# Forget-gate bias of eight attention heads: from prepared mask tiles on VectorE to one more accumulated matmul per score block on TensorE

## The chip, the cores and the metric

One Trainium2 chip, one of its cores. The metric is device microseconds of the whole program, the median of several runs. Engines are written as the profile writes them: PE is TensorE's matmul stream and PEld its weight load, DVE is VectorE, ACT is ScalarE, POOL is GpSimd, SP is SyncE.

## The reference, cut to what matters

The program is a four-layer model over 256 tokens of width 1024, in fp32: two layers of a first block (attention and a gated feed-forward each), then two layers of a second block with a mixture of experts. The change touches the first layer's attention alone. It has 16 heads of 64 columns: eight "dilated" heads whose bias is a constant table, and eight "forgetting" heads, whose bias depends on the data:

```python
def forgetting_attention(q, k, v, logf):
    c = jnp.cumsum(logf, axis=1)          # per token and head
    ck = jnp.transpose(c, (0, 2, 1))
    ...
        bias = jnp.transpose(cb, (0, 2, 1))[..., :, None] - ck[:, :, None, :]
        p = causal_block_probs(qb, k, start, bias)   # softmax(q.k + bias), causal
        return jnp.einsum('bqhd,...->...', p, v)
```

The term of the query's own token is the same along a softmax row and drops out, so the kernel needs only the row vector `-c` over the keys for each of the eight heads.

## The kernel before, in words

All weights stream once from memory in chunks of 128 x 2048 fp32 through a ring of three buffers. SP issues a chunk's load once the chunk three before it has been split. Each weight is split into a high part (ACT, line 350) and a low part (DVE, line 704), and `group` on PE forms each product from three fp32r matmuls (`product`, lines 1238 to 1242). The order of work on each engine is written out by hand, and the engines meet at semaphores.

The first layer's input projection runs in six groups g = 0..5 of two chunks (`projections`: ACT from line 414, DVE from 1087, PE from 1328). Between the two chunks of groups 1 to 4, PE transposes the finished query or key columns (`qk_transposes`, line 1312). The two score blocks of heads 0 and 1 start in group 5.

The forget-gate row vectors `f_w[4]` (8 heads on 8 partitions, 256 keys) are ready early: a scan on DVE at line 1075 signals `negc_ready`. Then, in groups 2 and 3, `forget_rows` on PE (line 1316) spreads four heads' rows over 128 partitions each: a matmul with one column of the identity, broadcast to 8 x 128, as stationary operand and `f_w[4]` as moving operand. `forget_masks` on DVE (line 1078) adds the constant causal mask and writes a 128 x 384 mask tile per head (lines 1084 and 1085). Those tiles lie in buffers that are free at that time.

Attention goes head by head, software-pipelined by hand. PE's `rest` (line 1380) does for head a: `scores(a + 2)`, `turn(a + 1)` (three transposes of the probabilities, line 1363), `values(a)` (lines 1372 to 1374). A head's scores are two blocks in one bank, 128 x 128 and 128 x 256, contracted over the head's 64 rows (line 1355). A head is on partitions 0..63 if even, 64..127 if odd (`head_rows`, line 1635). DVE's `scores` (line 758) adds the mask, negates and takes the row minimum in one operation per block (line 763); ACT's `softmaxes` takes the exponential and the row sum (line 396); DVE copies the turned probabilities (line 774) and scales the output (line 794). The same code serves the second attention layer (`attention(16, ...)`, 64 rows, values of 128 columns) and the second block's latent attention (96 rows, values of 64 columns).

An fp32 matmul stands in the profile as two rows, and so does its weight load; they are called two passes in what follows.

Of the kernel before, what the change touches and what calls it, by code (L numbers as in the profile page):

```python
# [20 lines left out]
ALU = mybir.AluOpType  # L21
# [3 lines left out]
P = 128  # L25
S = 256
# [85 lines left out]
def build(nc, x, stream, router, small, const, fgain, out):  # L112
    es = ExitStack()
    with es:
# [3 lines left out]
        def sem(name):  # L118
            return es.enter_context(nc.semaphore(name))
# [49 lines left out]
        f_w = [s[:, i * S:(i + 1) * S] for s, i in ((spare_c, 1), (spare_c, 2), (spare_s, 0), (spare_s, 1),  # L169
                                                    (spare_c, 0), (spare_s, 2))]  # L170

        rope_flat, stick_flat = (a[:, :, :].rearrange("p t d -> p (t d)") for a in (rope_a, sT))
        forget_mask = [zm[:, i, :] for i in range(4)] + [a[:, i * 384:(i + 1) * 384] for a in (rope_flat, stick_flat) for i in range(2)]

        spare_q = qk_tok[:, :, :].rearrange("p t d -> p (t d)")
        rw = spare_q[:, 0:384].rearrange("p (j n) -> p j n", j=24)
        rbig = spare_q[:, 512:512 + NT * NE].rearrange("p (t n) -> p t n", t=NT)
# [27 lines left out]
        h_ready, bank_done = sem("h_ready"), sem("bank_done")  # L205
        dve_step, act_step = sem("dve_step"), sem("act_step")
        qk_tok_ready, qk_tr, qkT_ready, v_ready = map(sem, ("qk_tok_ready", "qk_transposed", "qkT_ready", "v_ready"))
        rows_done, fmask_ready = sem("forget_rows_done"), sem("forget_mask_ready")
        f_z, f_neg, f_ln, negc_ready = map(sem, ("forget_z_ready", "forget_neg_ready", "forget_ln_ready", "neg_c_ready"))
        s_done, nm_ready, p_ready, p_tr, pT_ready, pv_done, o_done = map(sem, (  # L210
            "scores_done", "neg_max_ready", "probs_ready", "probs_transposed", "probsT_ready", "pv_done", "o_done"))
# [474 lines left out]
        def _(dve):  # L686
# [68 lines left out]
            def attention(first, n, masks, scale, dv, diff, between=None, score_bank=0, turned_bank=6):  # L755


                def scores(a):
                    dve.wait_ge(s_done, first + a + 1)
                    if a >= 2:  # L760
                        dve.wait_ge(p_ready, first + a - 1)
                    for t, lo, hi in ((0, 0, 128), (1, 128, 384)):
                        ins = nc.vector.tensor_tensor_reduce(  # L763
                            sm[:, a % 2, lo:hi], B[score_bank + a % 2][:, lo:hi], masks(a)[:, lo:hi], -scale, 3e38,
                            ALU.add, ALU.min, nmax[:, a, t:t + 1])
                    ins.then_inc(nm_ready, 1)

                def probs(a):
                    dve.wait_ge(p_tr, first + a + 1)
                    step[0] += 1  # L770
                    nc.vector.reciprocal(rden[:, a, :], den[:, a, :]).then_inc(dve_step, 1)
                    if a >= 2:
                        dve.wait_ge(pv_done, first + a - 1)
                    nc.vector.tensor_copy(prT[:, a % 2, :], B[turned_bank + a % 2][:, 0:384]).then_inc(pT_ready, 1)

                    if diff and a % 2:
                        dve.wait_ge(dve_step, step[0])
                        step[0] += 1
                        ts(rden[:, a, :], rden[:, a, :], lamb[:, 6:7], None, ALU.mult).then_inc(dve_step, 1)
                    scale_step[a] = step[0]  # L780

                def outputs(a):
                    dve.wait_ge(dve_step, scale_step[a])
                    dve.wait_ge(pv_done, first + a + 1)
                    if diff and a % 2:
                        dve.wait_ge(o_done, first + a)
                    for t in range(NT):
                        z = B[4 + a % 2][:, t * dv:(t + 1) * dv]
                        col = (a // 2 if diff else a) * dv
                        o = tok[:, t, col:col + dv]  # L790
                        if diff and a % 2:
                            ins = stt(o, z, rden[:, a, t:t + 1], o, ALU.mult, ALU.add)
                        else:
                            ins = ts(o, z, rden[:, a, t:t + 1], None, ALU.mult)
                    ins.then_inc(o_done, 1)

                scale_step = {}

                def start():
                    scores(0)  # L800
                    scores(1)

                def rest():
                    probs(0)
                    for a in range(n):
                        if a + 2 < n:
                            scores(a + 2)
                        if a + 1 < n:
                            probs(a + 1)
                        outputs(a)  # L810
                        if between is not None:
                            between(a)
                    dve.wait_ge(o_done, first + n)

                return start, rest
# [259 lines left out]
            nc.vector.tensor_tensor_scan(f_w[4], f_w[2], f_w[5], 0.0, ALU.mult, ALU.add)\  # L1075
                .then_inc(negc_ready, 1)

            def forget_masks(first):

                for i in range(first, first + 4):  # L1080
                    if i % 2 == 0:
                        dve.wait_ge(rows_done, i // 2 + 1)
                    rows = B[4 + i // 2 % 2][:, i % 2 * S:(i % 2 + 1) * S]
                    tt(forget_mask[i][:, 0:P], rows[:, 0:P], cs("causal", 0, P), ALU.add)
                    tt(forget_mask[i][:, P:384], rows, cs("causal", P, 384), ALU.add).then_inc(fmask_ready, 1)

            def projections(c0, qk_first, kinds, start, between=None):
                for g in range(6):
                    c = c0 + 2 * g
                    split(c + AHEAD)  # L1090
                    if g == 5:
                        start()
                    split(c + 1 + AHEAD)
                    if between is not None and g in (2, 3):
                        between(4 * (g - 2))
                    if g < 4:
                        kinds(g, qk_first + g, c + 1, 2 * (g % 2))

# [6 lines left out]
            def kinds1(g, n, c, banks):  # L1105
                rope(n, c, banks, *(("cos_q", "sin_q"), ("cos_k", "sin_k"))[g % 2])

            start, rest = attention(0, 16, lambda a: cs("dilated") if a < 8 else forget_mask[a - 8], 1.0, HD, False)
            projections(C_HYB, 0, kinds0, start, forget_masks)
            dve.wait_ge(fmask_ready, 8)  # L1110
            rest()
            nc.vector.engine_nop().then_inc(tok_ready, 2)
            low(T_L0O, xl, xh, one)
# [9 lines left out]
            dve.wait_ge(lam_exp, 1)  # L1123
            link(tt(lamb[:, 5:6], lamb[:, 3:4], lamb[:, 2:3], ALU.subtract))
            link(ts(lamb[:, 6:7], lamb[:, 5:6], -LAM_INIT, None, ALU.add))
            start, rest = attention(16, 16, lambda a: cs("causal"), 1.0, P, True, head_norms)
            projections(C_DIFF, 4, kinds1, start)
            rest()
            head_norms(17)
# [9 lines left out]
            for l in range(LAYERS):  # L1139
# [74 lines left out]
                        dve.wait_ge(spv_done, l + 1)  # L1214
                        nc.vector.tensor_copy(tok[:, :, 512:768], B[7][:, :].rearrange("p (t d) -> p t d", t=NT))

                start, rest = attention(32 + 8 * l, 8, lambda a: cs("chunked"), MLA_SCALE, HD, False, other_outputs, 2, 0)
                start()
                rest()
                nc.vector.engine_nop().then_inc(tok_ready, 2)  # L1220
# [14 lines left out]
        def _(pe):  # L1235
# [77 lines left out]
                                                  src[:, t, j * width:(j + 1) * width], ident)  # L1313
                    ins.then_inc(qk_tr, 1)

            def forget_rows(first):

                if first:
                    pe.wait_ge(fmask_ready, first)
                else:  # L1320
                    pe.wait_ge(negc_ready, 1)
                for i in range(first, first + 4):
                    row = ident[0:8, i:i + 1].broadcast_to([8, P])
                    ins = mm(B[4 + i // 2 % 2][:, i % 2 * S:(i % 2 + 1) * S], row, f_w[4], start=True, stop=True)
                    if i % 2:
                        ins.then_inc(rows_done, 1)

            def projections(c0, n0, q, start, between=None):
                for g in range(6):
                    if g == 1:  # L1330
                        pe.wait_ge(f_z, 1)
# [5 lines left out]
                    for j in group(c0 + 2 * g, 2, [B[b][:, :], B[b + 1][:, :]], 512, q if g == 0 else None):  # L1337
                        if j == 0 and 1 <= g <= 4:
                            qk_transposes(n0 + g - 1)
                        if j == 0 and g in (2, 3) and between is not None:  # L1340
                            between(4 * (g - 2))
                        if j == 0 and g == 5:
                            pe.wait_ge(qkT_ready, 2 * (n0 + 4))
                            pe.wait_ge(v_ready, n0 + 2)
                            start()

            def attention(first, n, operands, v_of, dv, between=None, score_bank=0, turned_bank=6):

                def scores(a):
                    if a >= 2:  # L1350
                        pe.wait_ge(nm_ready, first + a - 1)
                    o = B[score_bank + a % 2]
                    q, k = operands(a)
                    for lo, hi, t in ((0, 128, 0), (128, 384, 1)):
                        ins = mm(o[:, lo:hi], q[:, t * P:(t + 1) * P], k[:, 0:hi - lo], start=True, stop=True)  # L1355
                    ins.then_inc(s_done, 1)

                def turn(a):
# [277 lines left out]
                r = (a % 2) * HD  # L1636
                return qT[r:r + HD, a // 2, :], kT[r:r + HD, a // 2, :]

            start, rest = attention(0, 16, head_rows, lambda a, t: v[:, t, a * HD:(a + 1) * HD], HD)
            projections(C_HYB, 0, None, start, forget_rows)  # L1640
            pe.wait_ge(v_ready, 4)
            rest()
            pe.wait_ge(const_in, 16)
# [17 lines left out]
            for l in range(LAYERS):  # L1661
# [106 lines left out]
                def latent_heads(a):  # L1768
                    if a in (0, 4):
                        pe.wait_ge(qkT_ready, 2 * (n + (4 if a == 0 else 5)))  # L1770
                    return qT[0:MLA_QK, a, :], kT[0:MLA_QK, a, :]

                start, rest = attention(32 + 8 * l, 8, latent_heads, lambda a, t: v[:, t, a * HD:(a + 1) * HD], HD,
                                        other_mixers, 2, 0)
                start()
                qk_transposes(n + 4, MLA_QK, mla_tok[1])
# [192 lines left out]
```

## Time and profile before

| | us |
|---|---|
| runs | 1594.02, 1612.99, 1613.31 |
| median | 1612.99 |
| the profiled execution's own time | 1594.02 |
| span of the profile, first to last instruction | 1592.3 |
| what lies around the span | 1.7 |

The three runs lie in two places, 19 us apart, and the profiled execution is the shortest of them. A duration read from the profile belongs to that one.

The page's first part gives the busy time of each engine, its second part 40 slices of the span, its fourth the chain of work that ended last. A span with PE busy all through and a chain that lies on PE says that PE's own order of work sets the end there. Idle time of another engine in such a stretch costs nothing.

### The profile page before, as it was taken

The page shows a single profiled execution, that of the slowest core. Times are in us where ns is not written, and L with a number is a line of the kernel's source. Part 1 is how long each engine was busy: PE and PEld are TensorE (multiplying, and loading weights), DVE is VectorE, ACT ScalarE, POOL GpSimd, SP SyncE. Part 2 cuts the span into 40 slices and gives each one's busy share as a digit, 9 for nine tenths or more (in the row PEclk, how much of TensorE's full clock was granted, in tenths as well). Part 3 has the DMA queues.
Part 4 walks back from the last instruction along what each step waited for, and adds up shares of the span by engine and source line. Part 5 has one row for each costly group of instructions (what it writes and reads, how often), then busy time and mean ns, then how long its engine had stood idle before and what let it go on. Part 6 is the DMA issues. An engine that isn't in the chain of part 4 may idle for free.

```text
span 1592.3 us, 23360 instructions
## 1 busy us (share of the span) xinstructions
PE 1503.7 (94%) x8132; PEld 1272.6 (80%) x8132; DVE 1143.2 (72%) x1885; ACT 929.0 (58%) x1522; POOL 32.5 (2%) x68
## 2 busy tenths in 40 slices
PE   7999999999999999989879999999899799999997
PEld 5877999988778999977768887878678678787875
DVE  6665756667676656656668888889666578888886
ACT  5354554454555544547447767777555367776774
POOL 0000000000010000010000000000000000000000
PEclk9999999999999999989979999999997899999999
DMA  7422444545314454441318979799421359898984
GB/s 308 179 80 80 185 184 176 193 158 185 133 54 159 165 205 184 163 158 54 132 62 339 368 293 367 296 357 344 193 103 43 142 220 358 312 349 313 349 326 186
DMA packets 46828, 336.77 MB, mean 211 GB/s; under 512 B 5344, under 2 KB 5472, under 8 KB 6432
## 3 DMA queue, kind: packets, MB, share of 16 engines
q1 hardware_dynamic: 46656, 335.49, 56.0%
q8 instruction: 44, 0.72, 0.2%
q0 software_dynamic: 96, 0.30, 0.1%
q14 instruction: 32, 0.26, 0.1%
HBM read 334.72 MB, written 1.05 MB: 211 GB/s over the span
## 4 chain that ended last, share of the span: by engine, by line
PE 86%; DVE 6%; ACT 4%; issue 2%; POOL 1%; DMA 1%; DVEq 0%; ACTq 0%; SPq 0%; POOLq 0%
PE bank L1240 24%; PE bank L1242 23%; PE bank L1241 23%; DVE w_low L704 2%; PE bank L1355 2%; PE bank L1465 2%; PE bank L1476 2%; PE bank L1363 1%; ACT w_high L350 1%; PE bank L1508 1%; PE bank L1288 1%; ACT tok L360 1%; PE bank L1299 1%; PE bank L1312 1%; PE bank L1374 1%
## 5 line engine op out<-in xcount | busy, mean ns | idle before, releaser
L704 DVE TENSOR_TENSOR w_low<-raw,w_high 128x1024 fp32r<-128x1024 f32 (+2 forms) x630 | 734.7, 1212 | 189.9 <-ACT w_high L350 187.9
L350 ACT ACTIVATE w_high<-raw 128x1024 fp32r<-128x1024 f32 (+2 forms) x630 | 623.5, 1044 | 113.3 <-PE bank L1242 71.1
L1240 PE MATMUL bank<-w_high,x_high 128*128 128x512 f32 (+1 forms) x928 | 376.2, 405 | 8.4 <-DVE rope_b L975 3.1
L1242 PE MATMUL bank<-w_high,x_low 128*128 128x512 f32 (+1 forms) x928 | 364.0, 392 | 0.0
L1241 PE MATMUL bank<-w_low,x_high 128*128 128x512 f32 (+1 forms) x928 | 362.1, 390 | 0.0
L1240 PEld LDWEIGHTS bank<-w_high,x_high 128*128 128x128 f32 x928 | 175.7, 189 | 47.2 <-issue 9.1
L1242 PEld LDWEIGHTS bank<-w_high,x_low 128*128 128x128 f32 x928 | 175.5, 189 | 38.2
L1241 PEld LDWEIGHTS bank<-w_low,x_high 128*128 128x128 f32 x928 | 176.1, 190 | 34.4 <-issue 1.4
L1240 PE MATMUL bank<-x_high,w_high 128*128 128x256 f32 (+1 forms) x712 | 201.8, 283 | 1.0 <-DVE x_low L724 0.5
L1242 PE MATMUL bank<-x_high,w_low 128*128 128x256 f32 (+1 forms) x712 | 201.3, 283 | 0.0
L1241 PE MATMUL bank<-x_low,w_high 128*128 128x256 f32 (+1 forms) x712 | 201.3, 283 | 0.0
L1240 PE MATMUL bank<-w_high,hid_high 128*128 128x512 f32 x432 | 171.3, 397 | 1.9 <-DVE hid_low L979 1.9
L1241 PE MATMUL bank<-w_low,hid_high 128*128 128x512 f32 x432 | 170.6, 395 | 0.0
L1242 PE MATMUL bank<-w_high,hid_low 128*128 128x512 f32 x432 | 170.4, 394 | 0.0
L1240 PEld LDWEIGHTS bank<-x_high,w_high 128*128 128x128 f32 (+1 forms) x712 | 135.6, 190 | 3.8 <-DVE x_low L724 1.6
L1241 PEld LDWEIGHTS bank<-x_low,w_high 128*128 128x128 f32 (+1 forms) x712 | 135.6, 190 | 0.8
L1242 PEld LDWEIGHTS bank<-x_high,w_low 128*128 128x128 f32 (+1 forms) x712 | 135.6, 191 | 0.2
L1240 PEld LDWEIGHTS bank<-w_high,hid_high 128*128 128x128 f32 x432 | 81.4, 188 | 19.8 <-DVE hid_low L979 2.3
L1242 PEld LDWEIGHTS bank<-w_high,hid_low 128*128 128x128 f32 x432 | 81.4, 189 | 19.2
L1241 PEld LDWEIGHTS bank<-w_low,hid_high 128*128 128x128 f32 x432 | 81.5, 189 | 17.6
L396 ACT ACTIVATE probs<-scores_masked,neg_max 128x128 f32<-128x128 f32 x96 | 42.8, 446 | 55.6 <-DVE neg_max L763 55.5
L498 ACT ACTIVATE hid_high<-bank 128x256 fp32r<-128x256 f32 x64 | 24.6, 384 | 76.4 <-PE bank L1508 76.3
(244 smaller groups left out, 1434.5 us busy)
## 6 DMA issues: line engine op xcount, KB each, us to landing
raw<-stream SPq DMA_DIRECT2D x314, 1024.0 KB, 4.8
const_sb<-const SPq DMA_DIRECT2D x1, 2070.0 KB, 15.0
residual<-x SPq DMA_DIRECT2D x2, 512.0 KB, 4.3
final_gain<-fgain SPq DMA_DIRECT2D x2, 512.0 KB, 10.6
out<-residual SPq DMA_DIRECT2D x2, 512.0 KB, 2.6
small_sb<-small SPq DMA_DIRECT2D x1, 765.0 KB, 6.7
rope_a<-router POOLq DMA_DIRECT2D x2, 144.0 KB, 2.6
const_sb<-const SPq DMA_DIRECT2D x1, 136.0 KB, 4.5
```

The costliest lines, as they stand in the source:

```text
L350: nc.scalar.activation(wh[:, u, cols], raw[:, u, cols], ACT.Copy).then_inc(w_high, 1)
L360: nc.scalar.activation(tok[:, t, cols], h[:, t, cols], ACT.Square, scale=float(D) ** -0.5, accum_out=ssq[:, t, half:half + 1]).then_inc(ss ...
L396: ins = nc.scalar.activation(pr[:, a % 2, lo:hi], sm[:, a % 2, lo:hi], ACT.Exp, bias=nmax[:, a, t:t + 1], scale=-1.0, accum_out=den[:, a, ...
L498: nc.scalar.activation(gh[:, 0, :, 0:P], B[6][:, 0:2 * P].rearrange("p (k s) -> p k s", k=2), ACT.Copy)\
L704: ins = tt(wl[:, u, cols], raw[:, u, cols], wh[:, u, cols].bitcast(F32), ALU.subtract)
L1240: mm(o, ah, bh, start=start, stop=False, **kw)
L1241: mm(o, ah, bl, start=False, stop=False, **kw)
L1242: return mm(o, al, bh, start=False, stop=stop, **kw)
L1288: ins = nc.tensor.transpose(B[4 + b][:, at:at + P], tok[:, t, k * P:(k + 1) * P], ident)
L1355: ins = mm(o[:, lo:hi], q[:, t * P:(t + 1) * P], k[:, 0:hi - lo], start=True, stop=True)
L1465: ins = mm(B[2 + b][:, (k % 4) * P:(k % 4 + 1) * P], tok[:, t, k * P:(k + 1) * P], pick[:, t, g, :], start=t == 0, stop=t == NT - 1)
L1476: ins = mm(B[((5, 7), (2, 3))[half][t]][:, :], spread[:, g, t * P:(t + 1) * P], ys[:, half * 512:(half + 1) * 512], start=True, stop=True)
```

## The change

The mask tiles go. PE's `forget_rows`, DVE's `forget_masks` and the semaphores between them are removed from the projection. All 16 heads of the first attention now use constant masks in DVE's `scores`: `dilated` for heads 0 to 7, `causal` for 8 to 15. For heads 8 to 15, PE adds the row vector itself: each of the head's two score matmuls leaves its accumulation open, and a second matmul with the broadcast identity column (8 x 128) as stationary and `f_w[4]` (8 x 128 or 8 x 256) as moving operand closes it in the same bank. Before the scores of head 8, PE waits once for `negc_ready`. Other attention layers pass no `forget` and issue what they issued.

```diff
-        forget_mask = [zm[:, i, :] for i in range(4)] + [a[:, i * 384:(i + 1) * 384] for a in (rope_flat, stick_flat) for i in range(2)]
...
-                            sm[:, a % 2, lo:hi], B[score_bank + a % 2][:, lo:hi], masks(a)[:, lo:hi], -scale, 3e38,
+                            sm[:, a % 2, lo:hi], B[score_bank + a % 2][:, lo:hi], cs(masks(a), lo, hi), -scale, 3e38,
...
-            def forget_masks(first):
-
-                for i in range(first, first + 4):
-                    if i % 2 == 0:
-                        dve.wait_ge(rows_done, i // 2 + 1)
-                    rows = B[4 + i // 2 % 2][:, i % 2 * S:(i % 2 + 1) * S]
-                    tt(forget_mask[i][:, 0:P], rows[:, 0:P], cs("causal", 0, P), ALU.add)
-                    tt(forget_mask[i][:, P:384], rows, cs("causal", P, 384), ALU.add).then_inc(fmask_ready, 1)
...
-            start, rest = attention(0, 16, lambda a: cs("dilated") if a < 8 else forget_mask[a - 8], 1.0, HD, False)
-            projections(C_HYB, 0, kinds0, start, forget_masks)
-            dve.wait_ge(fmask_ready, 8)
+            start, rest = attention(0, 16, lambda a: "dilated" if a < 8 else "causal", 1.0, HD, False)
+            projections(C_HYB, 0, kinds0, start)
...
-            def forget_rows(first):
-
-                if first:
-                    pe.wait_ge(fmask_ready, first)
-                else:
-                    pe.wait_ge(negc_ready, 1)
-                for i in range(first, first + 4):
-                    row = ident[0:8, i:i + 1].broadcast_to([8, P])
-                    ins = mm(B[4 + i // 2 % 2][:, i % 2 * S:(i % 2 + 1) * S], row, f_w[4], start=True, stop=True)
-                    if i % 2:
-                        ins.then_inc(rows_done, 1)
...
-                        if j == 0 and g in (2, 3) and between is not None:
-                            between(4 * (g - 2))
...
+                    f = forget(a) if forget else None
                     for lo, hi, t in ((0, 128, 0), (128, 384, 1)):
-                        ins = mm(o[:, lo:hi], q[:, t * P:(t + 1) * P], k[:, 0:hi - lo], start=True, stop=True)
+                        ins = mm(o[:, lo:hi], q[:, t * P:(t + 1) * P], k[:, 0:hi - lo], start=True, stop=f is None)
+                        if f is not None:
+                            ins = mm(o[:, lo:hi], f, f_w[4][:, 0:hi - lo], start=False, stop=True)
                     ins.then_inc(s_done, 1)
...
+            def hybrid_heads(a):
+                if a == 8:
+                    pe.wait_ge(negc_ready, 1)
+                return head_rows(a)
+
+            start, rest = attention(0, 16, hybrid_heads, lambda a, t: v[:, t, a * HD:(a + 1) * HD], HD,
+                                    lambda a: ident[0:8, a - 8:a - 7].broadcast_to([8, P]) if a >= 8 else None)
+            projections(C_HYB, 0, None, start)
```

## Rows read from the trace of the kernel before

**Rows 1.** The page: its head, the engines' busy time, and the chain's shares by engine.

```profile
span 1592.3 us, 23360 instructions
PE 1503.7 (94%) x8132; PEld 1272.6 (80%) x8132; DVE 1143.2 (72%) x1885; ACT 929.0 (58%) x1522; POOL 32.5 (2%) x68
...
PE 86%; DVE 6%; ACT 4%; issue 2%; POOL 1%; DMA 1%; DVEq 0%; ACTq 0%; SPq 0%; POOLq 0%
```

**Rows 2.** Busy time by stretch: its length, engines (instructions), PE's granted clock, DMA.

```profile
18.00:88.00 70.00, 69.78 (x316) 57.15 (x318) 45.08 (x71) 31.19 (x38) 0.00 (x0) 0.98 0.55 203
...
108.00:124.00 16.00, 15.34 (x104) 12.08 (x104) 13.44 (x66) 8.17 (x34) 0.00 (x0) 1.00 0.01 2
```

**Rows 3.** Waits, 40 to 85 us: who for whom, total, times, longest.

```profile
DVE w_low L704 <- ACT w_high L350: 15.5, 5, 4.4
ACT w_high L350 <- PE bank L1242: 13.2, 3, 5.1
...
DVE qk_tok L752 <- PE bank L1242: 3.0, 2, 1.5
...
PEld bank L1240 <- issue: 0.7, 2, 0.3
PEld bank L1324 <- issue: 0.3, 2, 0.2
```

**Rows 4.** The chain that ended last, group 2 of the projection: start, length, what.

```profile
48.18 0.87 PE bank L1312 x8
49.05 1.92 PE bank L1324 x8
50.97 0.43 PE bank L1240
51.40 0.23 PE bank L1241
```

**Rows 5.** The same view, group 1, where no forget rows are made.

```profile
36.41 0.87 PE bank L1312 x8
37.28 0.23 PE bank L1240
```

**Rows 6.** Lines 1084 and 1085: duration ns min/median/max, first and last start.

```profile
L1084 DVE TENSOR_TENSOR stick_z<-bank,const_sb x4: 277/278/282, 53.0 to 54.6; 128x128 f32<-128x128 f32 x4
...
L1085 DVE TENSOR_TENSOR stick_z<-bank,const_sb x4: 410/410/411, 53.2 to 54.8; 128x256 f32<-128x256 f32 x4
```

**Rows 7.** The chain again, one turn of the first attention (64 rows).

```profile
109.63 0.85 PE bank L1355 x4
110.47 0.48 PE bank L1363 x3
110.96 0.17 PE bank L1372 x2
111.13 0.22 PE bank L1373 x2
111.35 0.22 PE bank L1374 x2
111.57 0.85 PE bank L1355 x4
```

**Rows 8.** Timeline of DVE, ACT and PEld in that turn.

```profile
110.51 0.29 DVE L763 CUSTOM_DVE_ANT_0 scores_masked<-bank,stick_z 128x128 f32<-128x128 f32 x1 [0.30 <-PE bank L1355]
...
110.04 0.19 ACT L396 ACTIVATION_READ_ACCUMULATOR probs<-scores_masked,neg_max 128x1 f32 x1
...
110.40 0.31 PEld L1363 LDWEIGHTS bank<-const_sb,probs 128*128 128x128 f32 x3 [0.33 <-ACT probs L396]
```

**Rows 9.** The chain, one turn of the second attention (64 rows, values 128 wide).

```profile
430.70 0.85 PE bank L1355 x4
431.55 0.48 PE bank L1363 x3
432.03 0.22 PE bank L1372 x2
432.25 0.22 PE bank L1373 x2
432.48 0.22 PE bank L1374 x2
432.70 0.85 PE bank L1355 x4
```

**Rows 10.** The chain, one turn of the latent attention (96 rows, values 64 wide).

```profile
759.26 0.33 PE bank L1363 x3
759.59 0.17 PE bank L1372 x2
759.76 0.22 PE bank L1373 x2
759.99 0.22 PE bank L1374 x2
760.21 0.71 PE bank L1355 x4
760.92 0.33 PE bank L1363 x3
```

**Rows 11.** By stretch as in rows 2: the low clock, and one latent-attention turn in it.

```profile
1212.78:1215.98 3.20, 3.20 (x14) 2.91 (x13) 1.74 (x8) 0.98 (x4) 0.00 (x0) 0.50 0.00 0
124.00:131.00 7.00, 6.14 (x30) 5.99 (x31) 2.50 (x9) 1.31 (x3) 0.00 (x0) 0.51 0.00 0
```

More of the change, by code:

```diff
@@ L170, in build @@
                                                     (spare_c, 0), (spare_s, 2))]
-        rope_flat, stick_flat = (a[:, :, :].rearrange("p t d -> p (t d)") for a in (rope_a, sT))
-        forget_mask = [zm[:, i, :] for i in range(4)] + [a[:, i * 384:(i + 1) * 384] for a in (rope_flat, stick_flat) for i in range(2)]
         spare_q = qk_tok[:, :, :].rearrange("p t d -> p (t d)")
@@ L207, in build @@
         qk_tok_ready, qk_tr, qkT_ready, v_ready = map(sem, ("qk_tok_ready", "qk_transposed", "qkT_ready", "v_ready"))
-        rows_done, fmask_ready = sem("forget_rows_done"), sem("forget_mask_ready")
+        rope_ready = sem("rope_ready")
         f_z, f_neg, f_ln, negc_ready = map(sem, ("forget_z_ready", "forget_neg_ready", "forget_ln_ready", "neg_c_ready"))
@@ L1076, in _, with projections @@
                 .then_inc(negc_ready, 1)
-            def forget_masks(first):
-                for i in range(first, first + 4):
-                    if i % 2 == 0:
-                        dve.wait_ge(rows_done, i // 2 + 1)
-                    rows = B[4 + i // 2 % 2][:, i % 2 * S:(i % 2 + 1) * S]
-                    tt(forget_mask[i][:, 0:P], rows[:, 0:P], cs("causal", 0, P), ALU.add)
-                    tt(forget_mask[i][:, P:384], rows, cs("causal", P, 384), ALU.add).then_inc(fmask_ready, 1)
-            def projections(c0, qk_first, kinds, start, between=None):
+            def projections(c0, qk_first, kinds, start):
                 for g in range(6):
@@ L1093, in projections @@
                     split(c + 1 + AHEAD)
-                    if between is not None and g in (2, 3):
-                        between(4 * (g - 2))
                     if g < 4:
@@ L1125, in _ @@
             link(ts(lamb[:, 6:7], lamb[:, 5:6], -LAM_INIT, None, ALU.add))
-            start, rest = attention(16, 16, lambda a: cs("causal"), 1.0, P, True, head_norms)
+            start, rest = attention(16, 16, lambda a: "causal", 1.0, P, True, head_norms)
             projections(C_DIFF, 4, kinds1, start)
@@ L1215, in other_outputs @@
                         nc.vector.tensor_copy(tok[:, :, 512:768], B[7][:, :].rearrange("p (t d) -> p t d", t=NT))
-                start, rest = attention(32 + 8 * l, 8, lambda a: cs("chunked"), MLA_SCALE, HD, False, other_outputs, 2, 0)
+                start, rest = attention(32 + 8 * l, 8, lambda a: "chunked", MLA_SCALE, HD, False, other_outputs, 2, 0)
                 start()
@@ L1314, in qk_transposes, with projections @@
                     ins.then_inc(qk_tr, 1)
-            def forget_rows(first):
-                if first:
-                    pe.wait_ge(fmask_ready, first)
-                else:
-                    pe.wait_ge(negc_ready, 1)
-                for i in range(first, first + 4):
-                    row = ident[0:8, i:i + 1].broadcast_to([8, P])
-                    ins = mm(B[4 + i // 2 % 2][:, i % 2 * S:(i % 2 + 1) * S], row, f_w[4], start=True, stop=True)
-                    if i % 2:
-                        ins.then_inc(rows_done, 1)
-            def projections(c0, n0, q, start, between=None):
+            def projections(c0, n0, q, start):
                 for g in range(6):
@@ L1339, in projections @@
                             qk_transposes(n0 + g - 1)
-                        if j == 0 and g in (2, 3) and between is not None:
-                            between(4 * (g - 2))
                         if j == 0 and g == 5:
@@ L1345, in projections, with attention @@
                             start()
-            def attention(first, n, operands, v_of, dv, between=None, score_bank=0, turned_bank=6):
+            def attention(first, n, operands, v_of, dv, forget=None, between=None, score_bank=0, turned_bank=6):
                 def scores(a):
@@ L1637, in head_rows @@
                 return qT[r:r + HD, a // 2, :], kT[r:r + HD, a // 2, :]
-            start, rest = attention(0, 16, head_rows, lambda a, t: v[:, t, a * HD:(a + 1) * HD], HD)
-            projections(C_HYB, 0, None, start, forget_rows)
+            def hybrid_heads(a):
[5 more added lines that the diff above has]
+            projections(C_HYB, 0, None, start)
             pe.wait_ge(v_ready, 4)
@@ L1771, in latent_heads @@
                     return qT[0:MLA_QK, a, :], kT[0:MLA_QK, a, :]
-                start, rest = attention(32 + 8 * l, 8, latent_heads, lambda a, t: v[:, t, a * HD:(a + 1) * HD], HD,
+                start, rest = attention(32 + 8 * l, 8, latent_heads, lambda a, t: v[:, t, a * HD:(a + 1) * HD], HD, None,
                                         other_mixers, 2, 0)
```

## The prediction

> **What bounds the kernel now.** I read the page first: PE is busy 94% of the span and the chain of work that ended last lies on PE for 86% of it [rows 1]. So the question is not how busy DVE is, but what PE itself does more or less of, stretch by stretch.
>
> Two stretches are touched. In the projection, 18 to 88 us, PE is busy for 69.78 of 70 us [rows 2]. The waits there are of DVE and ACT, for each other and for PE; PE waits for no other engine, only for 1.0 us of its own issue [rows 3]. DVE and ACT have slack, PE has none. The chain confirms it: it stays on PE through group 2 and through group 1 [rows 4, 5].
>
> In the heads, 108 to 124 us, PE is busy 15.34 of 16 us, DVE 13.44, and the clock is full [rows 2]. One turn takes 111.57 - 109.63 = 1.94 us: scores 0.85, transposes 0.48, values 0.61, all on PE [rows 7]. A row says that the transposes' weight load waited 0.33 us for ACT [rows 8]. I don't believe that ACT was the last: ACT's probabilities ended at 110.04 + 0.19 = 110.23, and the load began only at 110.40. The second attention settles it. There the values are 128 wide and take 0.66 instead of 0.61 us, and the turn is 2.00 instead of 1.94 [rows 7, 9]. A loop bound by the latency from scores through DVE and ACT back to PE passes that latency once in two turns and would not show the whole 0.05 in each. So PE's own list of work is the turn, and what is added to it is paid in full.
>
> What is the 0.33 then? The latent attention contracts over 96 rows and has the same work otherwise: its scores take 0.71 instead of 0.85, its transposes 0.33 instead of 0.48, and its turn 760.92 - 759.26 = 1.66 us [rows 10]. The 64-row heads pay 0.14 + 0.15 us more per turn. I read this as a price for going from 128 rows to 64 and back: PE runs empty before the other kind of matmul starts, and the weight load isn't hidden. The forget rows of the projection pay it too, with 8 rows. Eight passes at the 0.215 us which a 256-column pass takes (worked out below) are 1.72, the block takes 1.92, and the first product after it 0.43 instead of 0.23 [rows 4, 5]: 0.20 us at each end.
>
> **The change part by part.**
>
> Removed from PE: in each of groups 2 and 3, eight passes and two such ends. From rows: 1.92 + (0.43 - 0.23) = 2.12 us a group [rows 4, 5], two groups, 4.24 us. It all lies on the chain, PE has no slack there, so it all counts.
>
> Removed from DVE: eight adds of 128 x 128 at 0.28 us and eight of 128 x 256 at 0.41 (one start follows the other by less than these) [rows 6], 5.5 us busy. Worth nothing: DVE waits 15.5 us for ACT and 3.0 for PE in the same stretch [rows 3]. What is freed is more of that wait. The mask read in DVE's scores is as wide as before, so line 763 costs the same. The wait for `fmask_ready` never held anything, and the new one for `negc_ready` finds it raised some 80 us earlier; behind it on PE's queue stand the scores of head 8, and they aren't held. No DMA is moved: the chunk loads follow the splits, and those follow PE.
>
> Added to PE, eight heads long: per head one bias matmul of 128 columns and one of 256, two passes each. The pass prices: scores in the latent attention are two passes of each size in 0.71 us [rows 10]. The values and the transposes show 0.11 us a pass (0.22 for two, 0.33 for three [rows 10]), which I take for 128 columns; twice that, 0.215, for 256. Two of each make 0.645, which with the 0.06 of going from the narrow values to the scores gives the 0.71. Passes alone add 0.645 us a head.
>
> To that come the ends. The order is scores (64 rows), bias (8), scores (64), bias (8), then transposes (128). Before, a head had two changes of row count, now it has five: three more. No row shows 64 followed by 8. The bounds: below, 0, if PE treats 8 and 64 alike; above, 0.20 us each [rows 4, 5], and four of them if the last one before the transposes is dearer too. Between lie the 0.14 and 0.15 of the 64-row heads [rows 7, 10]. The nearest row is that of the very same bias matmul, with 0.20 at each end, so I take 3 x 0.20 = 0.60.
>
> A head becomes 0.645 + 0.60 = 1.245 us longer: its turn goes from 1.94 to 3.19. Eight heads: 9.96 us. DVE has 13.44 / 16 x 1.94 = 1.63 us of work a turn and ACT 0.99 [rows 2]; both wait longer for PE and don't become the bound.
>
> On this point the Trainium skill has a rule (TensorEngine Tiling, Key Properties): changing the tiling mode, not just the tile, drains TensorE, and its list of modes has 64 rows and 32 rows as different ones. By it each of the three changes costs a drain, as I have taken it; a reader who drops the rule is left with the range 0 to 0.20. No row here has 64 rows next to 8.
>
> The sum: -4.24 + 9.96 = +5.7 us on the profiled execution's own 1594.0 (span 1592.3, 1.7 around it), so 1599.7. With the bounds: +0.9 (0.645 x 8 - 4.24) to +7.3 (1.445 x 8 - 4.24). The profiled execution is the lowest of three runs, and the median is 19 us above. The change touches nothing that I can connect with these 19 us, so I carry the sum to the median: 1612.99 + 5.7 = 1618.7 us.
>
> **The rivals.**
>
> No price between 64 and 8 rows. The heads get 0.645 longer, 2.59 a turn, and the whole 0.9 us: 1613.9. For it: weight loads are hidden in every run of equal row count. Against: both changes of row count which the rows show, 128 with 64 and 128 with 8, cost.
>
> The odd heads' bias is free (the one that ends on the faster side). Heads 9, 11, 13 and 15 have their scores on partitions 64..127 and the bias lies on 0..7, so the two use different rows of the array and could run at the same time. Then only the even heads pay, 4 x 0.645 = 2.6, against 4.24 saved: -1.7 us, 1611.3. It decides once less than 4.24 / 8 = 0.53 us a head stays uncovered. Against it: both go to the same bank and columns, and the score turns of odd and even heads in the trace are equally long: the one in [rows 7], and those from 96 to 122 us repeat it within 0.01 us.
>
> The Trainium skill says that tiles of different row groups can execute in parallel (TensorEngine Tiling, Key Properties), and in the same list that a change of mode drains; no run of this trace pairs two such matmuls.
>
> The clock falls among the heads. After the last head's wait PE goes down to 0.51, 1.2 GHz, for 7 us, with both neighbours at full 2.4 GHz [rows 2, 11]. A latent turn at the low clock takes 3.20 instead of 1.66 us [rows 10, 11], so 1.54 more. A forget head would lose that and its bias passes' 0.645 again, plus some of its ends: about 2.5 us, 20 for eight heads: 1638.7. For it: PE runs empty five times a head instead of twice. Against it: the turns of 64-row heads ran at 1.00 throughout [rows 2].
>
> The low stretch after the heads doesn't come. It costs about 3 us of the 7 (6.14 busy, half of it [rows 11]); the denser heads before it or another phase could spare it: +5.7 - 3.1 = +2.6, 1615.6.
>
> **How the numbers follow.** Chances: forecast 0.60, no price between 64 and 8 rows 0.17, odd heads free 0.05, clock falls among the heads 0.07, low stretch spared 0.11. The likeliest case's own range is 1614 to 1621 if the runs fall where the median did. But they may fall where the profiled one did, 19 us lower, and then the same cases give 1592 to 1602. I give that 3 in 10. The range 1595 to 1624 holds the forecast in both places, leaves out the clock falling at the higher place (0.05), odd heads free and part of the no-price case at the lower (0.05), and some scatter, under 2 in 10 together.
>
> Faster or slower by over 2% (32 us, about what a measurement of this kernel can tell from no change) is reached by no case alone. Slower needs the fallen clock and a shift between the two places of the runs together: 0.04. Faster has no case, only the unknown: 0.01. Within 2%: 0.95.
>
> **What would show it.** Right: the chain in groups 2 and 3 goes from the transposes straight to a 0.23 us product, and the attention starts 4.2 us earlier. A turn of heads 8 to 15 is about 3.2 us, with PE busy through it, weight loads of the bias that start only after a gap, and longer waits of ACT and DVE for PE. Everything after 131 us is shifted by 5 to 6 us. Wrong: turns near 2.6 (changes are free), odd and even turns of unequal length (they overlap), or turns over 4 (the clock, which the same rows would show at 0.5). A shift after the attention that doesn't stay to the end would say that a later stretch isn't bound by PE.

## The result, and the profile after

The changed kernel takes 1622.2 us (median of 16 runs, 1615.5 to 1629.9), the kernel before 1593.2 (median of 16 runs, 1583.5 to 1613.7). The ratio is 1.0174, 95% interval 1.0147 to 1.0200: slower by 1.7%, some 28 us. Forecast was +5.7 us. The measured time lies in the stated range only because that range started from a median of 1613; over more runs the median of before is 1593. The forecast of the difference was wrong by a factor of nearly five, and the case that came true is the rival to which it gave 0.07.

The head of the page of the changed kernel, and PE's busy time, to be held against [rows 1]:

```profile
span 1618.9 us, 23376 instructions
PE 1532.1 (95%) x8148; PEld 1292.0 (80%) x8148; DVE 1139.9 (70%) x1869; ACT 928.7 (57%) x1522; POOL 32.6 (2%) x68
```

The chain that ended last in group 2 of the projection (start, length, what), for [rows 4]:

```profile
46.35 0.87 PE bank L1297 x8
47.22 0.23 PE bank L1225
```

The forget rows and the slow product behind them are gone, as in [rows 5]. Line 1297 is now `qk_transposes`, 1225 the first product. The chain again, the first turn with a bias, at head 8's prefetch:

```profile
101.59 0.41 PE bank L1327 x2
102.01 0.41 PE bank L1329 x2
102.42 0.63 PE bank L1327 x2
103.05 0.62 PE bank L1329 x2
103.67 0.48 PE bank L1337 x3
...
104.77 0.41 PE bank L1327 x2
```

104.77 - 101.59 = 3.18 us; 3.19 was predicted. Each of the four pieces of scores (1327) and bias (1329) has its 0.20 for a change of row count: 0.41 for two 128-column passes of 0.11, 0.63 for two of 0.215. But this is the only such turn. The same view, three turns later:

```profile
109.80 0.72 PE bank L1327 x2
110.52 0.72 PE bank L1329 x2
111.24 1.15 PE bank L1327 x2
112.39 1.15 PE bank L1329 x2
113.53 0.83 PE bank L1337 x3
...
115.54 0.72 PE bank L1327 x2
```

5.74 us a turn. The reason, from the busy time by stretch (length, engines, PE's granted clock in the third column from the right):

```profile
104.00:105.00 1.00, 1.00 (x10) 0.92 (x8) 1.00 (x6) 0.61 (x3) 0.00 (x0) 1.00 0.06 16
105.00:106.00 1.00, 1.00 (x5) 0.70 (x4) 0.35 (x2) 0.37 (x2) 0.00 (x0) 0.82 0.00 0
...
108.00:124.00 16.00, 16.00 (x50) 11.04 (x50) 5.14 (x24) 2.95 (x12) 0.00 (x0) 0.50 0.00 1
124.00:140.00 16.00, 16.00 (x50) 11.04 (x50) 5.22 (x24) 2.96 (x12) 0.00 (x0) 0.50 0.00 0
...
153.00:154.00 1.00, 1.00 (x5) 0.82 (x4) 0.79 (x3) 1.00 (x3) 0.00 (x0) 0.78 0.00 0
```

PE's clock falls from full (2.4 GHz) to half (1.2 GHz) at 105.65 us, in the second turn with a bias, and comes back at 153.4, when the dense products of the output projection run. Before, the stretch 108 to 124 was at 1.00 [rows 2].

Where the 26.6 us between the spans (1618.9 - 1592.3) come from, by marks in the chains of both traces. The first scores start at 81.66 instead of 87.75: -6.1, of which -4.2 for the rows. Most of the rest is the start of the projection: in the profile before, the clock was low from 18.2 to 21.6, and in this one it was not. From the first transposes of the heads to the first product of the output projection it is 151.85 - 89.37 = 62.5 us instead of 131.35 - 95.46 = 35.9: +26.6. Of these the bias itself at full clock is 8 x 1.24 = 9.9, the clock the other 16.7. The last +6.1 lie behind that. The slow start of the output projection has 0.8 of them. 4.5 come from a later place where the clock fell after PE's wait in a norm: from the start of that norm to the product behind the next `rope` it is 196.68 - 174.47 us now and 170.89 - 153.16 before. The rest is spread. The changed kernel's stretch:

```profile
176.00:188.00 12.00, 11.44 (x59) 11.20 (x60) 8.92 (x14) 7.09 (x12) 0.86 (x2) 0.57 0.09 23
```

Of the matmuls there, the 16 that clear the banks take 3.31 us, and 1.74 in the profile before, which passed the same wait at full clock. Such a fall comes in some executions and not in others: of the profiles taken for this study, only those of the changed kernel, `no_bias` and `changed_late_v` have it. The change doesn't touch that place.

### The profile page after: what moved, and what is told of

The parts are those of the page before. It is cut to its first block, busy times and chain, and to the rows that moved or that the text cites. A ratio compares the mean times of both kernels' runs of the same rounds, so it can differ in the third digit from the quotient of the medians.

```text
span 1618.9 us, 23376 instructions
## 1 busy us (share of the span) xinstructions
PE 1532.1 (95%) x8148; PEld 1292.0 (80%) x8148; DVE 1139.9 (70%) x1869; ACT 928.7 (57%) x1522; POOL 32.6 (2%) x68
## 4 chain that ended last, share of the span: by engine, by line
PE 86%; DVE 6%; ACT 4%; issue 2%; POOL 1%; DMA 1%; DVEq 0%; ACTq 0%; SPq 0%; POOLq 0%
PE bank L1225 23%; PE bank L1227 23%; PE bank L1226 23%; PE bank L1327 3%; DVE w_low L701 2%; PE bank L1439 2%; PE bank L1450 2%; PE bank L1337 1%; ACT w_high L347 1%; PE bank L1273 1%; PE bank L1482 1%; PE bank L1329 1%; PE bank L1284 1%; PE bank L1348 1%; PE bank L1347 1%
```

## The experiments

Three theories of why the clock falls among the heads. **A**: PE runs empty at each change of row count, five a turn. **B**: matmuls over few rows of the array, here 8 of 128, do it. **C**: something ahead of the heads does. Every run is compared with the kernel before on the same chip. Over all the experiments that kernel has 67 runs in two groups, 40 from 1582 to 1598 at a mean clock of 0.971 to 0.984, 26 from 1613 to 1616 at 0.958 to 0.962. One more took 1923, at a mean clock of 0.73, and stays unexplained. A median depends on how many fell in which group, so the groups are given where they matter.

### The bias left out

```diff
-                                    lambda a: ident[0:8, a - 8:a - 7].broadcast_to([8, P]) if a >= 8 else None)
+                                    None)
```

> The changed kernel without its sixteen bias matmuls: the forget rows and mask tiles are gone from the projection, and heads 8 to 15 get only the causal mask. It leaves the forget bias out of the output. Theory A (PE running empty at each change of row count lets the clock fall) and theory B (matmuls with 8 of 128 rows let it fall) both expect the clock at 1.00 through all sixteen heads, turns of 1.94 us, and -4.2 us against the kernel before (2.12 us in each of groups 2 and 3), with up to 3 us of scatter from the low stretch after the heads. Theory C (the clock falls at that place for a reason that lies ahead of the heads) expects it to fall here too, near 105 us, and a time some 10 us or more above before.

Measured: ratio 0.9985, interval 0.9935 to 1.0035. Four runs from 1585.8 to 1588.2, one at 1596.3, three from 1608.9 to 1609.9. The lower four are 5.7 to 8.2 us under the lower group's median of 1594.0, the upper three 4 us under the upper group's 1613.9. Two more runs took 3817 and 5187 us, at a clock of 1.00, and stay unexplained. In the profile the clock is at 1.00 through the heads, so C is out as the cause of what the changed kernel shows, and taking the rows out of the projection is worth the 4.2 us or slightly more:

```profile
91.00:119.00 28.00, 27.68 (x185) 21.97 (x185) 23.05 (x112) 13.35 (x54) 0.00 (x0) 1.00 0.10 38
```

The profiled run is the one at 1596.3; it has the later fall in the norm, with the same 3.31 us for the clearing matmuls.

### The same bias over 128, 64 and 32 rows

Each pads the two operands with zeros, in a tile `zm[:, 0, :]` cleared beforehand, and holds the rest as it is. For 128 rows:

```diff
-                            ins = mm(o[:, lo:hi], f, f_w[4][:, 0:hi - lo], start=False, stop=True)
+                            ins = mm(o[:, lo:hi], f, zm[0:128, 0, lo:hi], start=False, stop=True)
...
-                                    lambda a: ident[0:8, a - 8:a - 7].broadcast_to([8, P]) if a >= 8 else None)
+                                    lambda a: ident[0:128, a - 8:a - 7].broadcast_to([128, P]) if a >= 8 else None)
```

> The changed kernel with the bias operands padded with zeros to 128 rows: four changes of row count a turn (128, 64, 128, 64, 128) instead of five, and no matmul with few rows. This tells A from B. Theory A: the clock falls among heads 8 to 15 as in the changed kernel, a turn at the low clock near 5.5 us, and +15 to +25 us against before. Theory B: the clock stays at 1.00, a turn of 1.94 + 0.645 + 2 x 0.20 = 2.99 us, and 8 x 1.045 - 4.24 = +4.1 us.

Measured: 0.9994, interval 0.9946 to 1.0041; eight of ten runs from 1597.0 to 1603.4, one at 1627.9, one at 1927 (mean clock 0.73, like the odd run of the kernel before). Against the lower group (1594.0) that is +3 to +9, with +4.1 expected. The chain in its profile, and the stretch with its clock:

```profile
106.69 0.41 PE bank L1329 x2
107.11 0.42 PE bank L1331 x2
107.52 0.63 PE bank L1329 x2
108.15 0.63 PE bank L1331 x2
108.78 0.33 PE bank L1339 x3
...
109.72 0.41 PE bank L1329 x2
```

```profile
104.00:120.00 16.00, 16.00 (x90) 12.04 (x89) 8.04 (x42) 5.19 (x22) 0.00 (x0) 1.00 0.00 2
```

A turn of 3.03 us with four changes of row count, each at its 0.20 (the transposes, 0.33, now follow 128 rows and pay none), and a clock of 1.00. That speaks against A: PE runs empty nearly as often as in the changed kernel, and the clock holds. What is gone is the few rows and one of the five changes; the run with the bias first, below, has fewer changes still and settles A.

For 64 rows the operands lie on the head's own 64 partitions (`ident` and `zm` from `(a % 2) * HD` on, the row vectors copied to partitions 0 and 64).

> The changed kernel with the bias operands padded with zeros to 64 rows, on the head's own 64 partitions, so that scores and bias have one row count: two changes of row count a turn, as before, instead of five; the passes are the same. Theories A and B expect a turn of 1.94 + 0.645 = 2.59 us with the clock at 1.00, and 0.645 x 8 - 4.24 = +0.9 us against before. If the added passes themselves let the clock fall (theory C's kin), it is some 15 us more.

Measured: 1.0087, interval 1.0023 to 1.0151; three runs from 1596.4 to 1598.8, seven from 1615.6 to 1624.1. Not as expected, and the profile shows that this has another place. By stretch:

```profile
89.00:90.00 1.00, 0.44 (x3) 0.31 (x3) 0.00 (x0) 0.50 (x2) 0.00 (x0) 1.00 0.49 66
90.00:91.00 1.00, 1.00 (x6) 0.64 (x6) 0.63 (x3) 0.00 (x0) 0.00 (x0) 1.00 0.61 213
91.00:92.00 1.00, 1.00 (x8) 1.00 (x9) 1.00 (x6) 0.33 (x2) 0.00 (x0) 0.72 0.93 393
92.00:93.00 1.00, 1.00 (x5) 0.88 (x5) 0.56 (x3) 0.65 (x4) 0.00 (x0) 0.50 0.89 377
```

The clock fell at 91.45 us, 1.9 us behind the 1.2 us in which PE waits for ACT's copy of v at the entry to the heads, long before the first bias, and it stayed at 0.50 up to the output projection (156.3): a 64-row turn then takes 3.58 us instead of 1.94, and sixteen heads of them don't bring the clock back. That gave a new theory, **D**: this fall, in some executions only, is what lifts 26 of 67 runs of the kernel before by 20 us. It is taken up below.

For 32 rows, as for 128 with `[0:32]`:

> The changed kernel with the bias operands padded with zeros to 32 rows: the same changes of row count and the same passes as with 8 rows. Theory B1 (what counts is how many rows an instruction runs over, by degrees): 32 rows lie between 8, where every run fell, and 64, where three of ten didn't, so nearly all runs fall and a few may not; the median near +20 us. Theory B2 (8 rows is special): the clock stays as with 128 rows, and the time is +5.7 us or less. The 8 x 1.245 - 4.24 = +5.7 us of the prediction holds at full clock in either.

Measured: 1.0131, interval 1.0079 to 1.0183; all ten runs from 1614.0 to 1627.7. In the profile the clock falls at 107.1, in the second turn with a bias; where it fell in the other nine is known only from their mean clocks, 0.954 to 0.964. So 8 rows isn't special: the times of all runs with 8 and 32 rows show a fall, those with 128 hardly ever. No run has 33 to 63 rows, so whether the effect goes by degrees or has a step between 32 and 64 isn't shown.

### The bias first, in one matmul

```diff
+                    if f is not None:
+                        mm(o[:, 0:384], f, zm[0:8, 0, :], start=True, stop=False, skip_group_check=True)
...
-                        ins = mm(o[:, lo:hi], q[:, t * P:(t + 1) * P], k[:, 0:hi - lo], start=True, stop=f is None)
+                        ins = mm(o[:, lo:hi], q[:, t * P:(t + 1) * P], k[:, 0:hi - lo], start=f is None, stop=True,
```

> The changed kernel with the bias first: one matmul of 8 rows and 384 columns opens the bank, and both score matmuls accumulate onto it. Three changes of row count a turn (128, 8, 64, 128), the passes with 8 rows as long as in the changed kernel. Theory A: with one change more than before instead of three the clock has a fair chance to stay at 1.00; then a turn of 1.94 + 0.645 + 0.20 = 2.79 us and 8 x 0.845 - 4.24 = +2.5 us. Theory B: the clock falls, since the 8-row passes make up 0.23 of a turn instead of 0.20, and the time is +15 us or more.

Measured: four runs from 1615.1 to 1622.8, ratio 1.0125, interval 1.0048 to 1.0202. The first such turn starts at 103.34 and the clock is down at 104.4. With three changes of row count a turn the clock fell, and with four, over 128 rows, it held. A is out, B stands.

### The bias on every other head

```diff
-... if a >= 8 else None)
+... if a >= 8 and a % 2 == 0 else None)
```

> The changed kernel with the 8-row bias on heads 8, 10, 12 and 14 alone. It leaves the forget bias of the other four heads out of the output. Halves the share of 8-row passes over the eight heads, to about 0.13. If the clock follows the share over a few turns, it stays at 1.00 in some or all runs, and the lower runs lie at 4 x 1.245 - 4.24 = +0.7 us. If a single such head is enough, it falls at heads 8 to 10 and stays low: turns of 3.6 and 5.7 us in alternation, and about +15 us.

Measured: all ten runs from 1600.1 to 1609.4, median 1605.2 against 1591.8 for before's lower group: +13. (The ratio, 1.0011 with 0.9958 to 1.0064, is against both groups.) The clock falls at 109.4, in the second turn with a bias, and the chain then alternates:

```profile
110.19 1.58 PE bank L1327 x4
...
113.77 0.72 PE bank L1327 x2
114.49 0.72 PE bank L1329 x2
115.21 1.15 PE bank L1327 x2
116.36 1.15 PE bank L1329 x2
...
119.51 1.58 PE bank L1327 x4
```

3.58 and 5.74 us, as expected of "a few such heads are enough".

### The entry to the heads

`late_v` moves one wait of the kernel before. PE's first transposes and the scores of head 2 don't need v.

```diff
+                        if first == 0 and a == 0:
+                            pe.wait_ge(v_ready, 4)
                         values(a)
...
-            pe.wait_ge(v_ready, 4)
             rest()
```

> The kernel before with PE's wait for v moved from ahead of the first transposes of the heads to ahead of the first values: PE doesn't stand idle for the 1.2 us of ACT's copy between projection and heads. In bias_rows64 the clock fell in just that gap, ahead of any bias matmul, and stayed low through all sixteen heads. Theory D (that gap is what puts some runs of before 19 us above the others): the upper group of runs thins out or goes, and the median of before's kind falls to near the lower group, less about 1 us for the gap. Otherwise (the upper group has another origin) four in ten runs stay near 1613.

> late_v once more, for the count of runs: the four runs so far were all in the lower group, which chance alone gives in about one set of seven when 4 of 10 runs are in the upper one. Theory D expects no run above 1600 here. If the gap has nothing to do with it, about 4 in 10 are near 1613.

Measured: 4 and 12 runs, every one of them from 1583.2 to 1591.6; ratios 0.9888 (0.9795 to 0.9982) and 0.9970 (0.9943 to 0.9997). With 26 of 66 in the upper group, sixteen runs without one have a chance of (40/66)^16, under 1 in 1000. D is shown as far as this goes: with the gap gone, no run has the 20 us. No run of the kernel before from its upper group was profiled. What their mean clocks say fits: 0.014 less over 1613 us is some 45 us more at half speed (2 x 0.014 x 1613), an estimate, and fourteen of the 64-row turns at 3.58 us are 50. The chain at the entry, in `late_v`:

```profile
92.23 0.23 PE bank L1242
92.46 0.33 PE bank L1363 x3
92.79 0.85 PE bank L1355 x4
```

Before, 1.1 us of `ACT v` stood between them. Medians fall from the lower group's 1592.2 to 1589.5.

The same edit on two of the others:

> bias_rows64 with the wait for v moved. bias_rows64 had runs near 1597, 1615.6 and 1619 to 1624, and its profile showed the fall in the gap. If 64 rows are enough to keep the clock up once the gap is gone, all runs lie near 0.9 - 1.2 = -0.3 us from before's lower group, 1594. If 64-row bias passes let it fall as well, though more rarely than 8-row ones, part of the runs stay 15 to 20 us higher.

Measured: all ten runs from 1589.7 to 1597.2, ratio 0.9959 (0.9914 to 1.0005). The chain:

```profile
103.19 0.42 PE bank L1331 x2
103.61 0.22 PE bank L1333 x2
103.83 0.43 PE bank L1331 x2
104.26 0.43 PE bank L1333 x2
104.69 0.48 PE bank L1341 x3
...
105.79 0.41 PE bank L1331 x2
```

2.60 us a turn at a clock of 1.00, as the sum for "no change of row count" has it (2.59):

```profile
91.00:121.00 30.00, 30.00 (x200) 24.42 (x199) 20.85 (x104) 12.30 (x51) 0.00 (x0) 1.00 0.07 30
```

The bias (1333) over as many rows as the scores costs its passes and no more. Against 3.18 with three changes more, one change is (3.18 - 2.60) / 3 = 0.19 us. The Trainium skill's rule that changing the tiling mode drains TensorE (TensorEngine Tiling, Key Properties) is borne out by this and now has a price here.

Even so the padded form gains nothing over the mask tiles: with the same late wait these take 1589.5 (`late_v_again`), 3.6 us less than its 1593.1. In the two profiles 1.2 us of it is there early in the first feed-forward (ACT's `rope_a` on the chain starts at 165.64 against 164.45), where the sum has 0.9; the rest comes later, where the kernels do the same work.

> The changed kernel with the wait for v moved. The runs of the changed kernel lie near 1616 and near 1626; if the upper ones are those where the clock fell in the gap ahead of the heads, they go, and all runs lie near 1614, with the clock falling at heads 8 to 10 in each, because of the 8-row passes. If the late wait also kept the clock up under the 8-row passes, the time would be near 1598.

Measured: four runs from 1614.2 to 1622.4, ratio 1.0149 (1.0118 to 1.0180). The clock falls all the same, in the profile already in the first turn with a bias (at 102.85), so the gap isn't its origin:

```profile
103.00:119.00 16.00, 16.00 (x49) 10.89 (x48) 4.78 (x22) 2.96 (x12) 0.00 (x0) 0.50 0.00 0
```

That the upper runs of the changed kernel (1621 to 1630) are those of the gap isn't borne out: two of these four are at 1621.4 and 1622.4. The profiled run is the one at 1621.4, and it has the later fall in the norm, worth 4.5 us: without it, it would be at 1616.9, in the lower group. That accounts for this run; for those up to 1630 it isn't enough, and what else lifts them wasn't settled.

### A way to keep the 4.2 us

`dma_rows` leaves mask tiles and heads as before, but POOL stores `f_w[4]` to memory and loads each row back to all 128 partitions, straight into its mask tile; DVE adds the causal mask in place.

```diff
+            pool.wait_ge(negc_ready, 1)
+            pool.dma_start(row_store.ap(), f_w[4]).then_inc(rows_out, 16)
+            pool.wait_ge(rows_out, 16)
...
+                    pool.dma_start(forget_mask[i][:, P:384], row_store.ap()[i:i + 1, :].broadcast_to([P, S]))\
+                        .then_inc(rows_in[part], 16)
...
-            projections(C_HYB, 0, None, start, forget_rows)
+            projections(C_HYB, 0, None, start)
```

> The kernel before with the forget rows spread over the partitions by DMA (through a small store in memory, issued by POOL) instead of sixteen PE passes a group pair; DVE adds the causal mask to them in place, in groups 2 and 3 as before. No bias matmul in the heads. It tells whether the 4.24 us that the rows cost in the projection are there for the taking: -4.2 us against before, clock as before, both groups of runs (near 1594 and near 1613) 4 us lower. If a mask tile comes late, PE waits in group 2 or 3 and the gain is gone.

Measured: four runs from 1586.0 to 1591.3, median 1587.7 against the lower group's 1591.8: -4.1, as expected. The ratio, 0.9880 (0.9786 to 0.9974), is against both groups. PE is busy all through the projection:

```profile
18.00:84.00 66.00, 65.92 (x304) 54.45 (x304) 45.66 (x71) 31.12 (x38) 5.12 (x9) 0.97 0.65 232
```

That none of its four runs is in the upper group is too few to say anything: its entry gap is unchanged.

> dma_rows and late_v together on the kernel before: the forget rows spread by DMA, and PE's wait for v moved behind the first transposes. If the two gains add up, -4.2 and -1.2 us on the lower group of runs, and no upper group: every run near 1586, the median 5 to 8 us under before's lower group and 27 us under its upper one. If the gap was not the origin of the upper group, some of the runs lie near 1606.

Measured: six runs from 1585.1 to 1588.5, ratio 0.9956 (0.9939 to 0.9973), beside 0.9970 for `late_v_again`. The median, 1587.0, is 9.2 us under that of before on the same chip (1596.2) and 5.2 under its lower group. It is the fastest median of the study and beats both kernels. But the two gains didn't add up in full: over `late_v_again` it is 2.5 us, not 4.2. Its profile has the start of the projection at the low clock (0.97 from 18 to 86 us, 1.00 in that of `late_v_again`), which is worth about 2 us; whether that holds for all six runs isn't known.

## Why the prediction was right or wrong

**That PE bounds both stretches, so that passes count in full: right.** Nothing that DVE shed came back as time. One turn with bias at full clock took 3.18 us (3.19 predicted), one without changes of row count 2.60 (2.59), one with 128 rows 3.03 (2.99).

**The price of going between 64 and 8 rows: right.** It was bounded by 0 and 0.20 from rows that show 128 with 64 and 128 with 8, and taken at 0.20; measured 0.19. The rival of no price is out. So is that of odd heads running beside their bias: odd and even turns are equally long, 5.74 us each at the low clock (at full clock there is only the turn of head 8).

**The 4.24 us removed: right.** The product behind the transposes is back at 0.23, and `dma_rows` has -4.1.

**The clock: wrong, and this is the step that failed.** The prediction gave the fall among the heads 0.07, with the argument that 64-row turns ran at 1.00 throughout. It weighed only how often PE runs empty, and that isn't what decides, as bias_rows128 and bias_first8 show: what it put at nothing is the effect of the few rows, and that came to 16.7 us of the heads. The rows at hand didn't contain a stream of few-row passes: the projection's 8-row blocks stand between 128-row products for 1.92 us each. What should have given pause is in the same text: a price of 20 us for the rival against 5.7 for the forecast, with no row that speaks against it for 8 rows. Its price a head was right: 2.5 us at the low clock, measured 5.74 - 3.18 = 2.56. That the total for that case was close too, +25.7 predicted and some +28 measured, is partly luck: the first head with a bias still ran at full clock (16.7 instead of 20 us), and the fall in the norm, which has nothing to do with the change, made that up.

"PE busy 16.00 of 16.00" while the clock stands at half shows that the profile's busy share is no measure of what holds the clock. The Trainium skill (TensorE: Matmul & The Clock Gate, "What's actually happening") says that the gate is set by how busy PE has been recently. Taken as the profile's busy share, that would have kept the clock up here; the runs say that rows count too.

**The base: wrong.** "I carry the sum to the median" took two of three runs at 1613 for the rule. Of 67 runs 26 are there, and of the 16 beside the result four. The text said that the change touches nothing connected with these 19 us. By what `late_v` and the mean clocks show, both are the low clock through the heads, and where the changed kernel always has it, the 19 us can't come on top: 1613 + 5.7 added to a base that already had the low clock. The range held by luck: two errors of about 20 us, the base too high and the clock left out, offset each other. By the prediction's own figures, the fallen clock at the lower place of the runs is 1638.7 - 19 = 1619.7, inside the range and 2.5 us from what was measured; it had 0.07 x 0.3, some 0.02.

**The low stretch behind the heads: rightly named as open.** The prediction gave it 0.11 and some 3 us. It is there in the profiles of before, `no_bias` and `dma_rows`. In those of `bias_rows128` and of the four variants with the late wait and no few-row passes the clock is at 1.00 there. In the changed kernel the clock is low already when the heads end.

## What to carry to other kernels

A small matmul folded into a stream costs its passes, 0.2 us for each change of row count around it, and possibly the clock for the whole stretch. Pad its operands to the row count of its neighbours: 64 instead of 8 rows made 3.18 us a turn into 2.60 and, with the gap at the entry gone, kept the clock. Then compare the mended form with what it replaces: here its passes, 8 x 0.645 = 5.2 us, still cost more than the 4.2 of the mask tiles' rows. And where runs of one kernel lie in two groups, read each run's mean clock and look for a short wait of PE ahead of a stretch that can't win the clock back; moving one wait here took the upper group away.

## What the runs showed of the hardware that wasn't expected

- With passes over 8 or 32 rows among 64- and 128-row work, the times and mean clocks (0.953 to 0.970) of all 50 runs say that the clock fell (22 of the changed kernel and 4 of changed_late_v, 4, 10 and 10 of the variants). The five profiles among them show it within one or two turns. In runs with the gap at the entry, some may have fallen there already. With 64 rows and no gap it held in 10 of 10, with 128 rows in at least 8 of 10. The padding is zeros, so it is the rows the instruction runs over that count here, not data.
- Once low, it stayed low through work that holds it when high: 48 us in the changed kernel, and 65 us (91.45 to 156.3) with sixteen heads of 64 rows in bias_rows64. It came back only in the 128-row transposes and products behind the heads.
- Such a fall can also start at a wait of 1.2 us, in about 4 of 10 executions, and cost 20 us.
- The same wait is followed by a fall in one execution and by none in another: in the norm the chain lies off PE for the same 3.1 us, from 153.16 us before and from 174.47 after, with the clock full at its start both times, and only in the second does it fall (at 177.35). Nothing in the profiles ahead of it tells which will.
